# The wide product of a decoder trunk: four 512-column products, then four 256-column ones, in place of pairs

## The reference

```python
def conv_ffn(h, w_up, conv_w, conv_b, w_down):
    u = jnp.einsum('bsd,df->bsf', h, w_up)          # 2048 -> 2*5632
    S = u.shape[1]
    y = conv_b
    for tap in range(CONV_WIDTH):
        shifted = jnp.pad(u, ((0, 0), (tap, 0), (0, 0)))[:, :S]
        y = y + shifted * conv_w[CONV_WIDTH - 1 - tap]
    val, gate = jnp.split(y, 2, axis=-1)
    return jnp.einsum('bsf,fd->bsd', jax.nn.silu(gate) * val, w_down)   # 5632 -> 2048

for l in range(DEPTH):                               # DEPTH = 2
    h = rms_norm(x, mix_norm[l])
    x = x + (parallel_mixer if l % 2 == 0 else pool_mixer)(h, ...)
    h = rms_norm(x, ffn_norm[l])
    x = x + conv_ffn(h, w_up[l], conv_w[l], conv_b[l], w_down[l])
return rms_norm(x, final_norm)
```

## Time and profile before

| | |
|---|---|
| median of 3 runs | 1990.47 us |
| the three runs | 1988.1, 1990.47, 2003.0 us |
| span of the profiled execution | 1999.6 us |
| its device time | not shown beside the span |
| TensorE busy, share of the span | 98% |
| VectorE, ScalarE, GpSimd busy | 70%, 55%, 5% |
| mean DMA rate | 182 GB/s |
| wide stages, by the trace's clock | 458 to 1213 us and 1238 to 1980 us |

### The profile page before, as it was taken

How to read it: one execution, slowest core, us unless ns; L and a number is a source line. 1 busy time by engine, 2 the same in 40 slices (tenths; PEclk the granted TensorE clock), 3 DMA queues, 4 the chain that set the end, 5 groups by cost and what they waited for, 6 DMA issues and landing times.

```text
span 1999.6 us, 33329 instructions
## 1 busy us (share of the span) xinstructions
PE 1969.1 (98%) x11920; PEld 1753.1 (88%) x11920; DVE 1390.4 (70%) x2080; ACT 1097.7 (55%) x1809; POOL 109.0 (5%) x86
## 2 busy tenths in 40 slices
PE   8999999999999999999999999999999999999996
PEld 8899999998888888888888888888888888888885
DVE  7556765767777777777655556877787778755564
ACT  6444444555666555665544445666666566644443
POOL 2002240001000000000000011100000000000010
PEclk9999999999999999999999999999999999999999
DMA  7644554555555555554655544455555555555652
GB/s 265 223 167 162 176 169 151 187 170 186 183 183 185 188 189 189 182 181 162 210 190 189 183 161 161 169 189 189 189 189 189 189 189 189 189 184 174 210 189 84
DMA packets 186642, 364.92 MB, mean 182 GB/s; under 512 B 6435, under 2 KB 12108, under 8 KB 186572
## 3 DMA queue, kind: packets, MB, share of 16 engines
q1 hardware_dynamic: 181728, 358.64, 52.7%
q10 hardware_dynamic: 4844, 5.33, 0.8%
HBM read 361.83 MB, written 2.11 MB: 182 GB/s over the span
## 4 chain that ended last, share of the span: by engine, by line
PE 95%; DVE 3%; ACT 1%; DMA 0%; issue 0%; SPq 0%; DVEq 0%
PE ps L315 48%; PE ps L317 25%; PE ps L333 5%; PE ps L336 5%; PE ps L335 5%; PE ps L349 2%; PE ps L351 2%; PE ps L352 2%; DVE lo L908 1%; DVE h L915 1%; ACT hi L605 0%; PE ps L430 0%; ACT h L611 0%; DMA x<-in_xT 0%; ACT sqt L624 0%
## 5 line engine op out<-in xcount | busy, mean ns | idle before, releaser
L908 DVE TENSOR_TENSOR lo<-raw,hi 128x512 fp32r<-128x512 f32 x1360 | 953.4, 718 | 564.6 <-ACT hi L605 560.9
L605 ACT ACTIVATE hi<-raw 128x512 fp32r<-128x512 f32 x1356 | 846.0, 630 | 839.8 <-PE ps L317 644.8
L315 PE MATMUL ps<-h,hi 128*128 128x512 f32 x2816 | 987.0, 396 | 4.3 <-DVE lo L908 3.3
L317 PE MATMUL ps<-h,lo 128*128 128x256 f32 x2816 | 790.0, 281 | 0.0
L315 PEld LDWEIGHTS ps<-h,hi 128*128 128x128 f32 x2816 | 528.0, 188 | 129.7 <-DVE lo L908 4.9
L317 PEld LDWEIGHTS ps<-h,lo 128*128 128x128 f32 x2816 | 532.6, 189 | 0.0
L315 PE MATMUL ps<-act,hi 128*128 128x512 f32 x1408 | 492.9, 395 | 0.0
L317 PE MATMUL ps<-act,lo 128*128 128x256 f32 x1408 | 395.0, 281 | 0.0
L315 PEld LDWEIGHTS ps<-act,hi 128*128 128x128 f32 x1408 | 264.0, 187 | 61.9
L317 PEld LDWEIGHTS ps<-act,lo 128*128 128x128 f32 x1408 | 266.3, 189 | 0.0
L333 PE MATMUL ps<-h,hi 128*128 128x256 f32 x640 | 184.8, 289 | 7.4 <-DVE lo L908 7.2
(11 more groups left out here) (153 smaller groups left out, 1247.0 us busy)
## 6 DMA issues: line engine op xcount, KB each, us to landing
raw<-in_w_up SPq DMA_DIRECT2D x176, 1024.0 KB, 4.9
raw<-in_w_down SPq DMA_DIRECT2D x88, 1024.0 KB, 5.1
raw<-in_w_in SPq DMA_DIRECT2D x55, 1024.0 KB, 5.1
raw<-in_w_out SPq DMA_DIRECT2D x16, 1024.0 KB, 5.0
raw<-in_pool_w SPq DMA_DIRECT2D x4, 1024.0 KB, 5.2
out_T<-x ACTq DMA_DIRECT2D x4, 512.0 KB, 3.6
x<-in_xT SPq DMA_DIRECT2D x3, 512.0 KB, 9.5
raw<-in_w_in SPq DMA_DIRECT2D x4, 256.0 KB, 3.9
```

The lines of the kernel that those rows point to most:

```text
L315: pe.matmul(ps[:, bank + m, :], hi[:, kt, c], mv, start=first and kt == 0, stop=False, skip_group_check=True)
L317: mm = pe.matmul(ps[:, bank + m, S:2 * S], lo[:, kt, c], mv[:, 0:S], start=False, stop=last and kt == KT - 1, skip_group_check=True)
L605: a_.activation(hi[:, kt, :], raw[:, slot, kt, :], ACT.Copy).then_inc(hi_done, 1)
L908: ve.tensor_tensor(lo[:, kt, :], raw[:, slot, kt, :], hi[:, kt, :].bitcast(F32), ALU.subtract).then_inc(lo_done, 1)
```

## The change

The loop over the four blocks is split in two. The instructions, their operands, their number and their semaphores stay. The wait for `lo_done` stands ahead of the first product of the k-tile in both kernels, and the post of `w_used` at the last 256-column product.

```diff
                     for m in range(4):
                         c = slice(m * P, (m + 1) * P)
                         pe.matmul(ps[:, bank + m, :], hi[:, kt, c], mv, start=first and kt == 0, stop=False,
                                   skip_group_check=True)
+                    for m in range(4):
+                        c = slice(m * P, (m + 1) * P)
                         mm = pe.matmul(ps[:, bank + m, S:2 * S], lo[:, kt, c], mv[:, 0:S], start=False,
                                        stop=last and kt == KT - 1, skip_group_check=True)
                     mm.then_inc(w_used, 1)
```

## The result

The changed kernel took 2003.85 us in the median of 9 runs (2003.17 to 2006.35). Before took 1988.63 us in 9 runs (1988.07 to 2003.88), the three known ones among them. The ratio is 1.0059, interval 1.0036 to 1.0081: slower by more than its uncertainty, by less than the 1% bound. (The medians alone stand at 1.0077; the ratios given here weigh all runs, and before's two near 2003 pull this one down.) I had forecast 1988.4 us and no change.

The account below looks back on a forecast made before the run. TensorE's distance between product starts was taken to bound the kernel: the span of 1999.6 us less 13.6 us for the uneven pace, 1986.0, plus 2.4 around it gave 1988.4 us, range 1982 to 2007.

Parts of the forecast that it names:

- two paces of before: Wide product: pairs of 512 and 256 columns start 346.7 or 353.4 ns apart, kept until a stop of TensorE.
- third rival: Wide product: changing PSUM banks stalls TensorE, 84 us more if 20 ns were exposed, 2073 us; banks or clock 3%.
- second rival: Wide product: gaps close if the 26.7 ns over columns came from width changes, 85 us less, 1904 us; chance 4%.
- part on the change: Wide product: same instructions and waits, only the pace left; 1388 ns a k-tile, -13.6 us against the profiled execution.
- joints: Wide product: a k-tile's two changes of width, 512 to 256 and back, together cost 0.
- upper end: Wide product: width changes cost at most 6.7 ns a pair of them, +7.1 us over 1056 k-tiles.
- rows of one width: Trace rows of the narrow and token products: 120 ns per 256-column product, 227 ns per 512-column product.
- even pace: Wide product: pairs 346.7 ns apart, 1387 ns a k-tile; forecast for every wide k-tile, 79%.
- uneven pace: Wide product: pairs 353.4 ns apart, 1414 ns a k-tile, costing the profiled execution 13.6 us; cause unknown.
- first rival: Wide stages: the slower 353.4 ns pace stays; in part 1995 to 2010 us, 9%; in nearly all 2010 to 2017, 5%.
- sign of being wrong: Wide product: a k-tile clearly over 1390 ns with both rows at 227 and 120 would show unpriced costs.
- the sum had 2.4: Whole kernel: 2.4 us around the span, taken between 2.1 and 3.4, added to 1986.0 us.

Follow-up runs that it names:

- e1: Changed kernel, but all products of a k-tile after a group's first add into one PSUM bank instead of four; 2003.53 us.
- e2: Kernel before, widths still alternating, but each 256-column product belongs to the next block, so every product changes bank; 2015.96 us, ratio 1.0031.
- e7: Kernel before, with the narrow and token products reordered so that each writes another bank than the one before it; 2003.31 us, one run.
- e5: Changed kernel, but the four products with lo also take all 512 columns, so no 256-column product is left there; 2434.04 us, one run.
- e6: Changed kernel, but each 512-column product is made as two of 256 columns into the halves of its bank; 2057.36 us, one run.
- e12: Changed kernel's order in even k-tiles, its mirror (256s first) in odd ones, edited from before; 1998.42 us, ratio to before 0.9974.
- e10: Changed kernel, but with seven products of 512 columns and one of 256 in each k-tile; 2350.65 us, one run.
- e13: Changed kernel with no new edit, run in more rounds beside before on one chip; 2004.79 us, ratio 1.0069.
- e3: Kernel before, with widths going 512 256 256 512 512 256 256 512 except in a group's first k-tile; 1996.83 us, ratio 0.9938.
- e4: Kernel before, in blocks of two (twos): 512 512 256 256 512 512 256 256, except in a group's first k-tile; 1994.84 us, ratio 0.9923.
- e9: Kernel before, alternating, but with the 256-column product first in each pair; 1988.28 us, ratio 0.9937.
- e14: Kernel before with the 256-column product first in each pair, run again in more rounds on one chip; 1989.16 us, ratio 0.9987.
- e8: Kernel before, alternating, but the first k-tile of each group goes in blocks of two; 2007.33 us, ratio 1.0035.

## Why the prediction missed

**What held.** TensorE's spacing bounds the kernel, and the waits did not move (4.4 against 4.3 us). The two paces of before were read rightly: the sums of 1988.4 us for all even and 2016.5 for all uneven are the lowest and the highest place of its runs (of all of them the fastest took 1985.8, the slowest 2017.6 us), and the three given runs were two near the one and one near the middle place. The third rival, banks, was rightly held small: e1, e2 and e7 give it nothing. The clock didn't fall (granted 1.00 in the wide stages). The second rival was right to be refused: 13.3 ns over the columns' time stand on every product of one width, in e5 and e6 too.

**What failed** is one step of the part on the change: "A k-tile of four and four then takes 4 x 227 + 4 x 120 = 1388 ns", with the joints that "cost together 0 by that row" and +7.1 us at the upper end. The rows of one width hold only where no other width is near; e5 shows both at once. In a mixture most 512s that follow a 256 are 2 to 9 ns late, for five products (e12) or for a whole row of seven (first stretch of e10). The block order has four 512s in each k-tile, and all of them fall into that reach: in the trace of the changed kernel they are followed after 234.2, 234.6, 232.1 and 228.3 ns on average instead of 226.7, 22.5 ns too much in all. The 256s, at 118.5, give 6 back, and 16.6 are left, 17.5 us over 1056 k-tiles, against the 0 that I took and the 7.1 that I allowed. 1988.4 + 17.5 = 2005.9 us; measured 2003.85.

The reading behind the error: the even pace happened to equal the sum of the one-width rows (347 and 347), and I took that as proof that joints are free. They are not free there either, they cancel: 41 pairs of before between 1500 and 1514 us have 230 ns behind the 512 and 116.6 behind the 256, 3 late and 3 early. And with a second pace 6.7 ns away in the same code, the even one could speak for one pattern of joints only. The upper end should then have been the uneven pace for every product, 28.1 us. That figure did stand in the text, but as a rival, the uneven pace kept, not as the price of a new pattern.

**The first rival**, the uneven pace, did not come: the block order was at 1403.3 ns, or 1400 in one stretch of e13, whatever before drew. The time fell into the band that this rival was given for part of the execution (1995 to 2010 us, 9%), but by another mechanism, so that is luck. The sign of being wrong came in another form than written: a k-tile of more than 1390 ns, yes, but with the 512s at 232 and durations of 387 to 398 ns, not with both rows at 227 and 120.

**Smaller slips**, none of which changes the forecast. Every run of both kernels takes 1.7 to 1.8 us more than its span (2003.63 against 2001.8), where the sum had 2.4. With it the sum is 1987.8 us, and the profiled execution, 1999.6 us, was one of some 2001.4 us and none of the three given runs. And at 26.6 ns a k-tile 2010.4 us is crossed with some 830 uneven k-tiles, not 780.

**Is the change a loss?** Against a before that is mostly at its even pace yes: 15 to 16 us between the medians in two series, 0.8%, or 0.6 to 0.7% by the ratios, in which before's slower draws count too. Where before draws its middle place it is no loss, and e1, at the same pace as the changed kernel, was 0.999 (0.9953 to 1.0028) of a before with median 2004.05. The changed kernel itself was not run in that series, so a ratio for it there is argued, not shown.

**What stays open.** What makes the pattern isn't shown, nor why it changes across a stop, nor why before's odds differ from series to series (7 of 9 near 1988, then 3 of 31, then 22 of 26); that the chip decides is only suggested by the series' chips. e3, e4 and the block order show that the price goes with how the widths are arranged; why twos cost 7 ns a k-tile and fours 17 no run explains. That the product at which TensorE waits decides the odds of e9 and e14 is a guess; the order of the two products was changed, nothing else was tried.

**The version to take** is the alternating order with the 256s first. In the series that has both it takes 1989.16 us against 2004.79 of the changed kernel, 15.6 us less. It is level with before where before draws well and 0.6% shorter where it does not.

## What to carry to other kernels

Where an engine is at work for 98% of the time, divide the time from first to last start by the count, in several stretches, before any sum is made: two paces of one code mean that runs of before are a draw, and a median of three is one ticket. Don't price a mixture of sizes from rows that hold one size each; the nearest row has the same neighbours, some five products back or more. And a change that only reorders equal work can cost or give as much as a pace, here 16 us or 0.8%, with the waits and the shares of busy time all but unchanged.

## What the runs showed of the hardware

- A product in fp32r with its own load of weights is followed by the next after 120 ns (256 columns) or 226.7 ns (512), 13.3 ns over its columns at 2.4 GHz, without any spread: in the stretches read all durations are 389 ns in e5 and 283 in e6.
- Every steady pace of a k-tile is a multiple of 6.67 ns over the count of one or two k-tiles: 1386.7, 1393.3, 1400, 1403.3, 1413.3, 1726.7 and 1740 ns are 208, 209, 210, 210.5, 212, 259 and 261 times that, and 120 and 226.7 are 18 and 34 times.
- Where widths mix, most 512s within some five products of a 256 are 2 to 9 ns late and 256s next to a 512 up to 7 ns early (e10, e12, the changed kernel). One code can have two such patterns: alternating 346.7 or 353.4 ns a pair, fours 1400 or 1403 ns a k-tile (e1, e13), seven and one 1726 or 1740 ns (e10).
- A pattern lasts through some 500 k-tiles, from the up product into the down product, and through some 25 short changes of order (e8). In no trace here did a long stretch change its pace other than across a stop of TensorE.
- A change of PSUM bank between products costs nothing that these traces show, for either width: 1402 and 1399 ns a k-tile in one bank (e1) against 1403, 346.7 and 353.4 ns a pair with a change at every joint (e2), 227 and 120 ns in e7.
